# Seven block products for eight in the value panels of the dilated attention

## The reference

```python
z = u @ w_in
qk_m, v_m, o_m, gate_m, qkv_a, gates_br = split(z)
y_a = mlstm_branch(qk_m, v_m, o_m, gate_m, ...) @ w_a
y_b = dilated_attention(qkv_a, slopes) @ w_b
return (sigmoid(g_a) * y_a + sigmoid(g_b) * y_b) @ w_out
```

## Time and profile before

| what | us |
|---|---|
| median of 3 runs | 2273.26 (2271.74 to 2273.48) |
| span of the profiled execution | 2269.7 |
| its own time | not recorded beside the span |
| TensorE busy | 2229.6 |
| VectorE busy | 1432.9 |
| ScalarE busy | 488.6 |
| GpSimd busy | 286.7 |

### The profile page before, as it was taken

How to read it: one execution, slowest core, us unless ns; L and a number is a source line. 1 busy time by engine, 2 the same in 40 slices (tenths; PEclk the granted TensorE clock), 3 DMA queues, 4 the chain that set the end, 5 groups by cost and what they waited for, 6 DMA issues and landing times.

```text
span 2269.7 us, 30050 instructions
## 1 busy us (share of the span) xinstructions
PE 2229.6 (98%) x12022; PEld 1819.5 (80%) x12022; DVE 1432.9 (63%) x2592; ACT 488.6 (22%) x1067; POOL 286.7 (13%) x181
## 2 busy tenths in 40 slices
PE   7999999999999999999999999999999999999998
PEld 5888598799868885988998655588888887768987
DVE  5774355744656566756656777775575468766655
ACT  1212230100012222201010265321200023343300
POOL 0000011422000001213210000000000001001442
PEclk9999999999999999999999999999999999999999
DMA  9883338654576655465655411433433324445542
GB/s 392 296 301 132 112 131 315 228 181 143 203 276 193 246 186 204 155 233 186 195 196 175 170 38 38 158 112 130 146 134 129 118 96 167 131 167 186 177 167 84
DMA packets 179770, 398.77 MB, mean 176 GB/s; under 512 B 21168, under 2 KB 25648, under 8 KB 176560
## 3 DMA queue, kind: packets, MB, share of 16 engines
q1 hardware_dynamic: 136736, 285.03, 35.7%
q0 software_dynamic: 24080, 93.69, 11.9%
q10 hardware_dynamic: 18816, 18.12, 2.5%
HBM read 395.71 MB, written 1.11 MB: 175 GB/s over the span
## 4 chain that ended last, share of the span: by engine, by line
PE 92%; DVE 4%; DMA 1%; ACT 1%; issue 0%; POOL 0%; SPq 0%; DVEq 0%; ACTq 0%
PE bank L600 90%; PE bank L598 3%; DVE arena L2240 2%; DVE arena L2246 2%; DMA arena<-in_w_ada 1%; ACT arena L1540 1%; DVE junk L2246 0%; DVE arena L2243 0%; ACT L1540 0%; ACT arena L1543 0%; DVE arena L2836 0%; POOL arena L3472 0%; POOL arena L3474 0%; DVE arena L3238 0%; SPq L3408 0%
## 5 line engine op out<-in xcount | busy, mean ns | idle before, releaser
L600 PE MATMUL bank<-arena 128*128 128x256 f32 (+4 forms) x11438 | 2169.5, 357 | 17.2 <-DVE arena L2240 7.1
L600 PEld LDWEIGHTS bank<-arena 128*128 128x128 f32 (+2 forms) x11438 | 1753.4, 189 | 412.7 <-issue 224.8
L2240 DVE TENSOR_TENSOR arena<-arena 128x1024 f32<-128x1024 f32 (+6 forms) x567 | 476.6, 856 | 204.0 <-PE bank L600 170.2
L1540 ACT ACTIVATE arena<-arena 128x512 f32<-128x512 f32 (+5 forms) x443 | 222.6, 525 | 803.7 <-DVE arena L2240 471.1
L2246 DVE SCALAR_TENSOR_TENSOR arena<-arena 128x1028 f32<-128x1028 f32 (+6 forms) x367 | 317.0, 880 | 96.0 <-DMA arena<-in_w_ada 72.9
L2240 DVE TENSOR_TENSOR arena<-arena,bank 128x256 f32<-128x256 f32 (+2 forms) x382 | 171.8, 475 | 182.1 <-PE bank L600 171.1
L3504 POOL DMA_DIRECT2D arena<-in_w_ada x88 | 63.0, 716 | 1400.2 <-DVEq L2255 1354.0
L1540 ACT ACTIVATE arena<-bank 128x256 f32<-128x256 f32 (+1 forms) x129 | 53.0, 429 | 565.4 <-PE bank L600 564.8
L1543 ACT ACTIVATE arena<-bank 128x512 f32<-128x512 f32 (+1 forms) x163 | 88.4, 599 | 308.7 <-PE bank L600 270.4
L2240 DVE TENSOR_TENSOR arena<-bank,arena 128x512 f32<-128x512 f32 (+2 forms) x95 | 60.4, 646 | 127.7 <-PE bank L600 111.2
L2246 DVE SCALAR_TENSOR_TENSOR arena<-bank,arena 128x254 f32<-128x254 f32 (+2 forms) x184 | 78.1, 469 | 69.1 <-PE bank L598 35.4
(11 more groups left out here) (39 smaller groups left out, 272.3 us busy)
## 6 DMA issues: line engine op xcount, KB each, us to landing
arena<-in_w_ada POOLq DMA_DIRECT2D x88, 1028.0 KB, 5.9
arena<-in_w_in SPq DMA_DIRECT2D x84, 1024.0 KB, 7.4
arena<-in_w SPq DMA_DIRECT2D x56, 1024.0 KB, 7.2
arena<-in_w_mlp_in SPq DMA_DIRECT2D x32, 1024.0 KB, 7.3
arena<-in_w_mlp_out SPq DMA_DIRECT2D x32, 1024.0 KB, 7.0
arena<-in_w_gla SPq DMA_DIRECT2D x12, 1024.0 KB, 6.9
arena<-in_w_ada SPq DMA_DIRECT2D x16, 514.0 KB, 19.5
arena<-in_w_a SPq DMA_DIRECT2D x8, 1024.0 KB, 7.1
```

What stands on the lines that cost most here:

```text
L600: ins = nc.tensor.matmul(out, lhsT, rhs, start=start, stop=stop)
L1540: return nc.scalar.activation(out, x, f, **kw)
L2240: return V.tensor_tensor(out, x, y, op)
```

## The change

The three value panels of each layer go from six tiles of eight matmuls 128x512 to three panels of seven products, each of four matmuls 128x256 (`value_products`). So 32 matmuls of 256 columns' worth a panel become 28. The tokens are the stationary side, the weight blocks the moving one.

- TensorE: products 1 and 2 of pattern 0, `scores(0)`, the other five; of pattern 1 products 1, 2, 4, 5, then `turned(0)`, 7, 6, 3 and `scores(1)`; all seven of pattern 2, then `turned(1)` and `values(0)` as before.
- GpSimd: w5 and w7 of each value panel (`value_panel_sums`), in front of load 14 in layer 0 and of loads 43, 44 and 45 in layer 1. They share `gate_sum` with the gate panels, so the first gate panel's sums now wait for product 5 and w6 of pattern 2 and no longer only for the last head's S.
- VectorE: `token_sums("gates")` moves from behind the heads to in front of the last head's step (n = 11); pattern 0 uses these sums as well. `token_sums("classes")` is new, over every second token, for patterns 1 and 2. The weight sums w6 and w3, `first_sum` and `product_sums` of the three panels are put into the attention loop.
- ScalarE: six drains become three copies of 128x256.

```diff
+VALUE_JOBS = {14: [(0, 0), (0, 1), (0, 2)], 43: [(1, 0)], 44: [(1, 1)], 45: [(1, 2)]}
...
+        class_x = [UT[:, KH * j:KH * j + KH, r::RES] for j in range(2) for r in range(RES)]
+        class_tokens = {i: area(M["WORK"] + KH * P * j, KH, P) for j, i in enumerate((5, 6, 7, 4))}
...
-                def va(j, w):
...
+                def value_products(g, order):
+
+                    q = quarters(value_panel_at(l, g))
+                    x, sums, tag = value_tokens(g)
+                    ops = {1: (q[0], x[0]), 2: (q[1], x[2]), 4: (q[3], sums[4]), 5: (gate_sum, sums[5]),
+                           7: (q[2], sums[7]), 6: (q[0], sums[6]), 3: (q[1], x[3])}
+                    for i in order:
+                        key = f"VA {g} {i}"
+                        ps = open_tile(key)
+                        if i in (4, 5, 6, 7):
+                            pe.wait_ge(dve_done, DV.at(f"{tag} x{i}"))
+                        if i in (6, 3):
+                            pe.wait_ge(dve_done, DV.at(f"VA {g} w{i}"))
+                        if i in (5, 7):
+                            pe.wait_ge(value_sums_made, values_made(l, g, i))
+                        for k in range(KH):
+                            mm(ps[:, :2 * P], ops[i][1][:, k, :], ops[i][0][:, k, :], start=(k == 0), stop=(k == KH - 1),
+                               done=key if k == KH - 1 else None)
...
-                        for j in range(6):
-                            pe.wait_ge(act_done, AC.at(f"VA {j} drained"))
+                        for g in range(NPAT):
+                            pe.wait_ge(dve_done, DV.at(f"VA {g} c12"))
...
                 w = panel()
-                va(0, w)
+                value_products(0, ORDER[:2])
                 scores(0)
-                va(1, w)
+                value_products(0, ORDER[2:])
                 release(w)
                 w = panel()
-                va(2, w)
+                value_products(1, ORDER[:4])
                 turned(0)
+                value_products(1, ORDER[4:])
+                release(w)
                 scores(1)
-                va(3, w)
-                release(w)
                 w = panel()
-                va(4, w)
-                va(5, w)
+                value_products(2, ORDER)
                 release(w)
...
-                va(0)
+                first_value(0)
                 exponentials_of(0)
-                va(1)
-                va(2)
+                first_value(1)
                 turned(0)
-                exponentials_of(1)
-                va(3)
-                va(4)
-                va(5)
+                exponentials_of(1, (0,))
+                first_value(2)
+                exponentials_of(1, (1,))
...
                 for n in range(12):
+                    if n == 11:
+                        token_sums("gates", up_x, [gate_tokens[i] for i in (5, 6, 4)], False, gate_tokens[7])
...
-                token_sums("gates", up_x, [gate_tokens[i] for i in (5, 6, 4)], False, gate_tokens[7])
+                def value_weight_sums(g):
+
+                    dve.wait_ge(value_sums_made, values_made(l, g, 7))
+                    panel_sums(f"VA {g}", value_panel_at(l, g), 6, f"VA {g} 1", gate_sum)
+                    panel_sums(f"VA {g}", value_panel_at(l, g), 3, f"VA {g} 2")
...
+                dve.wait_ge(pe_done, PE.at(f"HT {M_HEADS - 1} full"))
+                token_sums("classes", class_x, [class_tokens[i] for i in (5, 6, 4)], False, class_tokens[7])
+                value_weight_sums(0)
+                first_sum("VA 0", value_blocks(0), value_read(0))
...
+                    if u == 0:
+                        for _ in product_sums("VA 0", value_blocks(0), value_read(0)):
+                            pass
+                    if u == 1:
+                        value_weight_sums(2)
+                        first_sum("VA 2", value_blocks(2), value_read(2))
...
+                    if u == 0:
+                        value_weight_sums(1)
+                        first_sum("VA 1", value_blocks(1), value_read(1))
+                        for _ in product_sums("VA 1", value_blocks(1), value_read(1)):
+                            pass
+                    if u == 1:
+                        for _ in product_sums("VA 2", value_blocks(2), value_read(2)):
+                            pass
...
+            def value_panel_sums(l, g):
...
+                if g:
+                    pool.wait_ge(pe_of[f"layer {l}"], PE.of(f"layer {l}", f"VA {g - 1} 5 full"))
+                    pool.wait_ge(dve_of[f"layer {l}"], DV.of(f"layer {l}", f"VA {g - 1} w6"))
+                else:
+                    pool.wait_ge(pe_of[f"layer {l}"], PE.of(f"layer {l}", "S 3 full"))
+                nc.gpsimd.tensor_tensor(gate_sum, a21, a22, ALU.add).then_inc(value_sums_made, 1)
+                pool.wait_ge(value_sums_made, values_made(l, g, 5))
+                nc.gpsimd.tensor_tensor(a21, a11, a21, ALU.subtract).then_inc(value_sums_made, 1)
```

More of the change, by code:

```diff
@@ L287, in program @@
         gate_sums_made = sem("gate_sums_made")
+        value_sums_made = sem("value_sums_made")
         mlp_sums_made = sem("mlp_sums_made")
@@ L511, in program, with value_panel_at, values_made, value_tokens @@
         UP = [(name, p) for p in range(5) for name in ("W1", "W3")]
+        def value_panel_at(l, g):
+            return gate_first[l] - 6 + 2 * g
+        def values_made(l, g, i):
+            return 2 * (NPAT * l + g) + (1 if i == 5 else 2)
+        class_x = [UT[:, KH * j:KH * j + KH, r::RES] for j in range(2) for r in range(RES)]
+        class_tokens = {i: area(M["WORK"] + KH * P * j, KH, P) for j, i in enumerate((5, 6, 7, 4))}
+        def value_tokens(g):
+            return (class_x, class_tokens, "classes") if g else (up_x, gate_tokens, "gates")
+        def value_blocks(g):
+            return {(i, m): VA[:, m - 1, PW * g + 2 * P * (i - 1):PW * g + 2 * P * i] for i in (1, 2) for m in (1, 2)}
         spare_sum = area(M["SIG"] + 1024, KH, 2 * P)
@@ L1711, in _, with first_value, exponentials_of @@
                         act_mini(h, s)
[L1712 to L1720, removed]
+                def first_value(g):
+                    act.wait_ge(pe_done, PE.at(f"VA {g} 1 full"))
+                    func(value_blocks(g)[1, 2], tile(f"VA {g} 1")[:, :2 * P], ACT.Copy).then_inc(
+                        act_done, AC.drained(f"VA {g} 1"))
+                def exponentials_of(u, heads=(0, 1)):
+                    for n in [2 * u + e for e in heads]:
                         act.wait_ge(dve_done, DV.at(f"slot negmax {n}"))
@@ L2822, in gate_panel, with value_read @@
                         pass
-                token_sums("gates", up_x, [gate_tokens[i] for i in (5, 6, 4)], False, gate_tokens[7])
+                def value_weight_sums(g):
+                    dve.wait_ge(value_sums_made, values_made(l, g, 7))
+                    panel_sums(f"VA {g}", value_panel_at(l, g), 6, f"VA {g} 1", gate_sum)
+                    panel_sums(f"VA {g}", value_panel_at(l, g), 3, f"VA {g} 2")
+                def value_read(g):
+                    return lambda i: tile(f"VA {g} {i}")[:, :2 * P]
+                dve.wait_ge(pe_done, PE.at(f"HT {M_HEADS - 1} full"))
+                token_sums("classes", class_x, [class_tokens[i] for i in (5, 6, 4)], False, class_tokens[7])
+                value_weight_sums(0)
+                first_sum("VA 0", value_blocks(0), value_read(0))
                 for u in range(SLOTS // 2):
@@ L3455, in gate_weight_sums @@
                 else:
-                    pool.wait_ge(pe_of[f"layer {l}"], PE.of(f"layer {l}", "S 3 full"))
+                    pool.wait_ge(pe_of[f"layer {l}"], PE.of(f"layer {l}", f"VA {NPAT - 1} 5 full"))
+                    pool.wait_ge(dve_of[f"layer {l}"], DV.of(f"layer {l}", f"VA {NPAT - 1} w6"))
                 nc.gpsimd.tensor_tensor(gate_sum, a21, a22, ALU.add).then_inc(gate_sums_made, 1)
@@ L3459, in gate_weight_sums @@
                 nc.gpsimd.tensor_tensor(a21, a11, a21, ALU.subtract).then_inc(gate_sums_made, 1)
+            def value_panel_sums(l, g):
+                n = value_panel_at(l, g)
+                a11, a12, a21, a22 = quarters(n)
+                for m in (n, n + 1):
+                    pool.wait_ge(panel_in[m % RING], 16 * (m // RING + 1))
+                if g:
[6 more added lines that the diff above has]
+                nc.gpsimd.tensor_tensor(a21, a11, a21, ALU.subtract).then_inc(value_sums_made, 1)
             def mlp_sums():
@@ L3494, in _ @@
                     value_sums((n - 74) // 4)
+                for job_ in VALUE_JOBS.get(n, ()):
+                    value_panel_sums(*job_)
                 for job_ in GATE_JOBS.get(n, ()):
```

## The result

The changed kernel takes 2279.6 us (median of 6 runs, 2277.49 to 2281.94), the one before, run beside it, 2273.1 (2271.72 to 2273.48): ratio 1.0028, 95% interval 1.0017 to 1.0038, so 6.4 us slower. The prediction was 2278.5. The profiled execution took 2277.49 with a span of 2275.7, so 1.8 us lie around a span.

A forecast was written before the change was run, and what follows sets the result against it. TensorE, busy 98% of the span, was taken to bound the kernel, with VectorE overfull in layer 1. Layer 0 at -0.7 and layer 1 at +4.9 gave +4.2, or +6.2; the middle, 2273.3 + 5.2 = 2278.5 us, range 2269.5 to 2281.5.

The forecast's parts named there:

- The saving: Value stages: 21 products take TensorE 36.4 us instead of 41.2, saving 4.8 us a layer, 9.6 in all.
- The bank wait: Second value panel, both layers: product 3 waits for product 4's bank until three sums free it, 1.4 us.
- The lock in layer 0: Behind VA 2: probability scalings take turns with GpSimd's gate sums, so values(0) starts 2.7 us later; layer net -0.7.
- Layer 1: Layer 1 value stage: VectorE holds 49.4 us of work for 46.1, so TensorE waits and the saving can't be had.
- first scores end 1.75 later: Layer 1: if GpSimd sums also hold the two-element negated maxima, the first scores end 1.75 us later.
- The 0.6 in front of product 7: Layer 1, VA 2: TensorE waits 0.6 us more for GpSimd's w7, whose sums stand behind load 44.
- the sum: Layer 1 total: -4.8 saved and 5.6 of waits give +0.8; with scalings held, values(0) 4.1 later, +4.9.
- the middle: Both layers: +5.2 us, taken between net +4.2 and +6.2, the latter with two-element scalings held too.
- the upper end: Both layers: net +6.2 us, if GpSimd sums hold the two-element scalings (negated maxima) as well.
- A: Both layers: GpSimd sums don't lock scalings; -3.4 + 0.8 = -2.6, 2270.7 us; chance 22%.
- B: Layer 1's VectorE queue is not the limit, both layers pay only the bank wait; -6.8, 2266.5 us; chance 10%.
- C: Class sums, stride of two elements, run at half speed on VectorE, 2.75 more; +8, 2281.3 us; chance 10%.

The follow-up runs named there:

- experiment 4: Changed kernel, with layer 0's turned(0) after two products of the second panel instead of four; 2278.22 us, ratio 1.0019.
- experiment 1: Changed kernel, with the first gate panel's GpSimd sums waiting for slot 3's scaled probabilities in both layers; 2274.32 us, ratio 1.0002.
- experiment 6: Changed kernel, with three turns moved behind layer 1's attention, and the places of the GpSimd sums with them; 2270.65 us, ratio 0.9999.
- experiment 2: Changed kernel, with layer 1's GpSimd sums for VA 2 put in front of load 44; 2279.01 us, ratio 1.0029.
- experiment 8: Changed kernel, with gate sums behind the scalings, turned(0) after two products in both layers and three layer 1 turns moved later; 2262.13 us, ratio 0.9956.
- experiment 5: Kernel before with the change in layer 0 alone, plus gate sums behind the scalings and turned(0) after two products; 2268.02 us, ratio 0.9985.

## Why the prediction was right

**The saving** (4.8 us a layer) holds: with every wait gone layer 0's stage is 4.9 and layer 1's 4.5 shorter, and the whole kernel gained 10.0 to 10.7.

**The bank wait** (1.4) is there in both layers at 1.43, and taking it away in layer 0 made the stage 1.7 shorter (experiment 4).

**The lock in layer 0.** Named was: GpSimd, one scaling, GpSimd, three scalings, `values(0)` 2.7 later, in all -0.7. The order was as laid out, and the stage is 0.9 shorter. Experiment 1 gives the lock's price, 2.3. So three terms, forecast as -4.8 + 1.4 + 2.7 and measured as -4.9 + 1.7 + 2.3, add up in both cases; the small misses have opposite signs.

**Layer 1.** Product 6 of VA 0 waited 1.51 (said 1.2), product 5 of VA 2 1.90 (said 1.8). Experiment 6 shows that without the turns both waits are gone. The 1.30 in front of VA 1's product 1 has no term in the sum. It is the held negated maximum: 1.86 instead of 0.17 puts the drain of `scores(0)` off. The prediction had the cause ("first scores end 1.75 later"), and not the bank that hangs on it. The 0.6 in front of product 7 can't be read here, since TensorE ran at its lower clock (below); in experiment 4, at full clock, it is 0.48. `values(0)` comes 7.2 us later; the sum had 4.9, or 6.9 with two-element scalings held.

**The term that was mis-sized** is that choice. The text kept +4.2 and +6.2 and took the middle, 5.2. The small scalings are held, so the upper end was the right one; medians give +6.5, the ratio +6.4. By it the forecast would have been 2279.5. That size doesn't protect was already in the earlier trace rows, where three sums of 128x8 took 3.13. The middle had no mechanism behind it, and that it missed by only 1.1 us is no credit to it. No run takes the hold off the small scalings alone; an estimate from the lines is 1.30 (the wait for the bank) and 0.55 (slot 2's, as in experiment 2), against the 2.0 of the text.

**The rivals.** A fell with experiment 1. B, VectorE no limit in layer 1, fell on the waits there. Experiment 6 shows that VectorE is no limit once the turns are away; even then the two stages are only 1.7 us shorter than before by the traces and not 6.8, since B also needed scalings that aren't held. C fell on one row: the four class sums and w6 and w3 took 5.21, of which w6 and w3 are 2.55, so 0.67 a class sum, against 0.69 for one without stride. The Trainium skill (SBUF — State Buffer, Door 1: The DMA port swizzle) calls steps of up to four fp32 elements free, and the trace agrees for a step of two.

**Not settled:** how much of layer 1's 7.6 each single wait is worth. From turn 42 to `values(0)` the waits all hang on one VectorE queue without idle time, and experiment 2 shows that taking one away makes the next longer. Experiment 4 shows the same: its layer 1 is the changed kernel's code but behind the 1.9 in front of product 5 it waits 0.48 and 2.21 where the changed kernel waits 1.26 in one piece, and the stage is as long to 0.1 us.

## What to carry to other kernels

Work taken off TensorE is worth its time only where the engine that receives the sums has room: add up that engine's stretch first, and look for work that can leave it. The 49.4 us of work for 46.1 named layer 1 as the layer that loses, and three turns moved out of it were worth 7 to 9 us, while they were worth nothing before the change. Between GpSimd's SBUF sums and VectorE, ask for each start which VectorE instruction comes next and who waits for it; one wait moved behind four scalings gave 5 us by the medians, and 3.9 in the two stages by the traces. And where a bank is taken again behind a short piece of work, a piece placed two products earlier removed the wait.

## What the runs showed of the hardware that was not expected

**The clock after a wait.** Granted clock (the third column from the end) of TensorE in the changed kernel, layer 1, a stretch of 1 us behind the wait of 1.90, and the first of full clock:

```profile
894.00:895.00 1.00, 1.00 (x4) 0.80 (x3) 0.97 (x2) 0.94 (x3) 1.00 (x1) 0.50 0.58 234
...
897.00:898.00 1.00, 1.00 (x6) 0.88 (x5) 1.00 (x1) 0.31 (x2) 0.94 (x1) 1.00 0.08 16
```

TensorE had waited 1.43 at 881 and 1.90 at 892; with the restart the clock fell to its lower level (1.2 GHz), and it was back at 2.4 GHz before 897. Four products took 8.83 where as many records at 868.19 took 7.16, 1.7 more. Here it cost nothing, since `turned(1)` had to wait 1.26 for the scalings anyway. In experiment 2 the clock fell behind the waits of 1.71 and 2.58, and the transposes took 3.60 against 1.92. That cost nothing either. VectorE's last product sums of VA 2, and TensorE's `values(0)`, in experiment 2:

```profile
905.38 2.52 DVE L2266 TENSOR_TENSOR arena<-arena,bank 128x256 f32<-128x256 f32 x6
```
```profile
908.11 18.98 PE L621 MATMUL bank<-arena 128*64 128x256 f32 x184
```

`values(0)` starts 0.21 behind the end of the sums, as in the changed kernel (906.82 and 907.03), where the transposes ran at full clock. The next heading has a spell that did cost time. The kernel before had such spells elsewhere (its mean clock is 0.996 as well), none in this stage. In layer 1 of experiments 6 and 8 the clock stayed full.

**Two groups of times about 7 us apart.** The single times of some kernels fall into two groups: in experiment 8, 2259.5 to 2263.5 (four) and 2268.3 to 2269.4 (two); in experiment 5, 2265.3 to 2271.0 (eight) and 2274.0 to 2274.9 (three); in experiment 6, 2269.2 to 2273.6 (nine) and 2277.0 to 2278.2 (three). The profiles of 8 and 6 are from the longer group, that of 5 from the shorter. TensorE behind the mixer of layer 0, the transposes for its MLP and the products behind them, in 8 and then in 5; the last fence is 6:

```profile
421.38 1.11 PE L619 MATMUL bank<-arena 128*128 128x128 f32 x4 [6.47 <-DVE arena L2270]
422.29 3.62 PE L621 MATMUL bank<-arena 128*128 128x512 f32 x4
```
```profile
417.00 0.66 PE L621 MATMUL bank<-arena 128*128 128x128 f32 x4 [1.54 <-DVE arena L2321]
417.50 1.88 PE L623 MATMUL bank<-arena 128*128 128x512 f32 x4
```
```profile
426.13 1.11 PE L619 MATMUL bank<-arena 128*128 128x128 f32 x4 [6.58 <-DVE arena L2269]
```

In the other eight traces this wait is 1.4 or less.

VectorE in front of it, in 8 and then in 5 (a pair of 128x1 operations follows, 2.38 and 0.35):

```profile
416.14 1.91 DVE L2267 TENSOR_TENSOR arena<-arena 128x1 f32<-128x1 f32 x1
```
```profile
415.55 0.16 DVE L2318 TENSOR_TENSOR arena<-arena 128x1 f32<-128x1 f32 x1
```

GpSimd, in 8 and then in 5:

```profile
415.70 2.34 POOL L3497 TENSOR_TENSOR arena<-arena 128x1024 f32<-128x1024 f32 x1 [3.83 <-DMA arena<-in_w]
```
```profile
416.37 2.79 POOL L3551 TENSOR_TENSOR arena<-arena 128x1024 f32<-128x1024 f32 x1 [5.09 <-DMA arena<-in_w]
```

A weight sum of the MLP starts when its half panel lands. In 8 it starts 0.4 us ahead of VectorE's three one-element operations, and they take 4.3 us instead of 0.5; in 5 it starts behind them, and in 6 it is again 0.4 ahead. TensorE waits 4.9 longer in 8 than in 5. Behind that wait its clock is at 1.2 GHz until about 426 us, while in 5 it stays at 2.4, and this takes another 2.4 (from the first transpose to the next stretch 5.1 against 2.7). Together they make 7.4, against 7.8 and 7.2 between the means of the groups. So the medians of 5, 6 and 8 hold a mixture, and differences by the lengths of stages are the surer ones. Only the traces of 6 and 8 show the longer group, and no run was made to move the sum and test it.
